# Turned input, normalization behind the products, and a first block with k outermost

## The reference

```python
h = x
proj = rmsnorm(h, norm_mix_g) @ w_in          # 512 x 1024 @ 1024 x 4624
y_a = gmlp_chunk_mixer(proj[:, :2048], ...)   # gelu, per-head rmsnorm of v, 128x128 causal mixing, rmsnorm
y_b = ssd_mixer(proj[:, 2048:], ...)          # z | x,B,C -> causal conv (4 taps) -> silu | dt -> softplus; scan
h = h + concat([y_a, y_b]) @ w_out
h = h + square(relu(rmsnorm(h, norm_mlp_g) @ w_ff1)) @ w_ff2
h = h + sigmoid(rmsnorm(h, ple_norm_g) @ w_gate) * (p @ w_ple)
out = rmsnorm(h, final_norm_g)

rmsnorm(x, g) = x * rsqrt(mean(x * x) + eps) * g
```

## Time and profile before

| | us |
|---|---|
| median of 3 runs (733.01 to 733.64) | 733.08 |
| span of the profiled execution, first to last instruction | 731.3 |
| median less span (what lies around the span) | 1.8 |
| PE busy | 721.8 |
| DVE busy | 528.3 |
| ACT busy | 410.3 |
| POOL busy | 134.1 |
| start of the first matmul of block 0 | 10.99 |
| granted TensorE clock, mean | 0.997 |

### The profile page before, as it was taken

How to read it: one execution, slowest core, us unless ns; L and a number is a source line. 1 busy time by engine, 2 the same in 40 slices (tenths; PEclk the granted TensorE clock), 3 DMA queues, 4 the chain that set the end, 5 groups by cost and what they waited for, 6 DMA issues and landing times.

```text
span 731.3 us, 9961 instructions
## 1 busy us (share of the span) xinstructions
PE 721.8 (99%) x3962; PEld 622.3 (85%) x3962; DVE 528.3 (72%) x552; ACT 410.3 (56%) x521; POOL 134.1 (18%) x112
## 2 busy tenths in 40 slices
PE   8999999999999999999999999999999999999996
PEld 7888887778887888888899889988999889988884
DVE  5556795477658555555889985899579967898874
ACT  6534456653576762413767742774447625673875
POOL 1021000756645000001110211212111121020000
PEclk9999999999999999999999999999999999999998
DMA  8632222343233153219667898889978997887311
GB/s 330 205 105 86 87 87 89 115 151 109 86 111 120 60 201 116 73 43 285 151 170 211 178 296 159 218 192 295 206 180 222 221 250 156 235 177 260 115 58 58
DMA packets 52229, 118.24 MB, mean 162 GB/s; under 512 B 5052, under 2 KB 5208, under 8 KB 52184
## 3 DMA queue, kind: packets, MB, share of 16 engines
q1 hardware_dynamic: 39816, 84.03, 34.4%
q0 software_dynamic: 11136, 29.36, 22.1%
q10 hardware_dynamic: 1232, 4.23, 1.8%
HBM read 96.60 MB, written 4.23 MB: 138 GB/s over the span
## 4 chain that ended last, share of the span: by engine, by line
PE 97%; DMA 1%; DVE 1%; ACT 1%; issue 0%; SPq 0%
PE acc L1651 28%; PE acc L1653 28%; PE acc L1652 28%; PE side L1716 3%; PE side L1651 2%; PE side L1652 2%; PE side L1653 2%; PE side L1809 2%; PE side L1776 1%; DMA w_raw<-in_w_in 1%; PE side L1816 1%; PE side L1804 1%; DVE w_lo L1108 0%; PE side L1756 0%; PE side L1757 0%; PE side L1796 0%
## 5 line engine op out<-in xcount | busy, mean ns | idle before, releaser
L767 ACT ACTIVATE ring_hi<-quarter 128x1024 fp32r<-128x1024 f32 x112 | 113.6, 1051 | 101.9 <-PE acc L1653 46.5
L1409 DVE TENSOR_TENSOR ring_lo<-quarter,ring_hi 128x1024 fp32r<-128x1024 f32 x112 | 132.8, 1219 | 38.0 <-ACT ring_hi L767 37.7
L1651 PE MATMUL acc<-w_hi,a_hi 128*128 128x512 f32 x256 | 104.4, 408 | 0.1
L1653 PE MATMUL acc<-w_hi,a_lo 128*128 128x512 f32 x256 | 100.1, 391 | 0.0
L1652 PE MATMUL acc<-w_lo,a_hi 128*128 128x512 f32 x256 | 99.8, 390 | 0.0
L648 POOL DMA_DIRECT2D quarter<-in_w_ff x24 | 29.2, 1236 | 240.4 <-DMA quarter<-in_w_ff 240.2
L1652 PE MATMUL acc<-xS_lo,ring_hi 128*128 128x256 f32 x256 | 72.4, 283 | 0.0
L1108 DVE TENSOR_TENSOR w_lo<-w_raw,w_hi 128x1024 fp32r<-128x1024 f32 x36 | 48.0, 1336 | 27.1 <-ACT w_hi L669 26.7
L1651 PEld LDWEIGHTS acc<-w_hi,a_hi 128*128 128x128 f32 x256 | 48.1, 188 | 11.5 <-issue 1.4
L1652 PEld LDWEIGHTS acc<-w_lo,a_hi 128*128 128x128 f32 x256 | 48.2, 188 | 10.7 <-issue 1.4
L1653 PEld LDWEIGHTS acc<-w_hi,a_lo 128*128 128x128 f32 x256 | 48.0, 188 | 10.4
(11 more groups left out here) (290 smaller groups left out, 1817.7 us busy)
## 6 DMA issues: line engine op xcount, KB each, us to landing
quarter<-in_w_ff SPq DMA_DIRECT2D x72, 512.0 KB, 5.8
w_raw<-in_w_in SPq DMA_DIRECT2D x36, 512.0 KB, 3.7
quarter<-quarter POOLq DMA_DIRECT2D x32, 512.0 KB, 8.0
quarter<-in_w_ff POOLq DMA_DIRECT2D x24, 512.0 KB, 7.4
w_raw<-in_w_out SPq DMA_DIRECT2D x16, 512.0 KB, 3.5
h<-in_x SPq DMA_DIRECT2D x8, 512.0 KB, 4.7
seg<-cs_dram ACTq DMA_DIRECT2D x8, 512.0 KB, 3.8
w_raw<-in_w_ple_gate SPq DMA_DIRECT2D x8, 512.0 KB, 5.7
```

Of the source, the lines that this page charges most:

```text
L767: act.activation(ring[n % 3][0][at], quarter[i][at], ACT.Copy).then_inc(form_hi, 1)
L1409: dve.tensor_tensor(lo[at], src, hi[at].bitcast(F32), ALU.subtract).then_inc(form_lo, 1)
L1651: pe.matmul(dst, st[0], mv[0], start=start, stop=False)
L1653: return pe.matmul(dst, st[1], mv[0], start=False, stop=stop)
```

## The change

x comes a second time from DRAM, turned (channels on partitions), into the space of `y`, eight pieces of 128 channels by 512 tokens, and `norm_mix_g` as a small tile with one gain for each channel (`g_col`). a_hi and a_lo are made from these two with no turning on PE and no token factor. The token factors come from x as before, into `rstd`, and are applied behind the products: as the scale of gelu and silu in blocks V, U and Z, and in blocks 2 to 4 by a DVE multiplication with a tile `rstd_row` that holds them along the free dimension on every partition. That tile is made by one matmul of ones by four diagonal matrices behind group 4, and copied out by ACT at t = 6. Block 0 runs with k as the outer loop over its four banks. ACT issues the first three weight pieces of block 0, SP the other five and the eight of x turned. WARM is 11, REWARM is gone; `ones` is set by DVE.

```diff
+            for k in range(KT):                                    # SP
+                sp.dma_start(xt_raw[:, k, :], xt_dram[:, k, :]).then_inc(xt_landed[k], 16)
+                if k == 0:
+                    sp.dma_start(g_col[:], a["norm_mix_g"]).then_inc(g_col_landed, 16)
+                if k >= ACT_FIRST:
+                    sp.dma_start(w_raw[:, k // 2, k % 2, :], w_in[:, k, W:W + 512]).then_inc(first_landed[k], 16)
+            for s in range(NS):
+                load_x(s)
...
+            for k in range(ACT_FIRST):                             # ACT
+                act.dma_start(w_raw[:, k // 2, k % 2, :], w_in[:, k, W:W + 512]).then_inc(first_landed[k], 16)
             act.wait_ge(eps_ready, 1)
             act.activation(early_rms[:], eps[:], ACT.Sqrt).then_inc(sqrt_loaded, 1)
+            act.wait_ge(g_col_landed, 16)
+            for k in range(KT):
+                split_xt(k)      # a_hi[:, k, :] = xt_raw[:, k, :] * g_col[:, k]
+                split_first(k)   # w_hi[:, 0, k, :] = w_raw
+            for s in range(NS):
+                sums(0, s)
+            for p in range(4):
+                split_hi(1, p)
...
+                if t == 6:
+                    freed(act.activation(rstd_row, wait_full(act, "rstd_row"), ACT.Copy), "rstd_row")
...
-                    act.activation(conv[:, i % 2, :], acc[:, s, :], ACT.Copy, scale=cols[:, 36 + i:37 + i]
+                    act.wait_ge(*emptied(b, s))
+                    act.activation(conv[:, i % 2, :], tmp[:, i % 2, :], ACT.Copy, scale=cols[:, 36 + i:37 + i]
                                    ).then_inc(conv_begun, 1)
-                    act.wait_ge(*emptied(b, s))
+                    act.wait_ge(conv_step, 3 * i + 3)
...
+            for k in range(KT):                                    # DVE
+                split_xt(k)      # a_lo
+                split_first(k)   # w_lo
+            dve.wait_ge(consts_ready, 2)
+            for s in range(NS):
+                dve.wait_ge(rms_ready, s + 1)
+                dve.reciprocal(rstd[:, s:s + 1], rms[:, s:s + 1]).then_inc(rstd_ready, 1)
+                dve.wait_ge(rstd_ready, s + 1)
+                dve.tensor_scalar(rstd_diag[:, s, :], ident[:], rstd[:, s:s + 1], None, ALU.mult
+                                  ).then_inc(diag_ready, 1)
+            for p in range(4):
+                split_lo(1, p)
...
             for t in range(4 * OUT):                               # DVE
                 b, s = divmod(t, 4)
-                if 1 <= t < 3:
-                    xt_evac(0, t + 1)
+                if 5 <= t < 9:
...                      # the v_ssq reduction, moved to the head of the iteration
+                if t == 11:
+                    bank = wait_full(dve, "dt")
+                    freed(dve.tensor_tensor(dtT[:], bank[0:2 * R, :], rstd_row[0:2 * R, :], ALU.mult), "dt")
+                if X <= b < U:
+                    i = t - 4 * X
+                    dve.wait_ge(acc_full, t + 1)
...
+                    dve.tensor_tensor(tmp[:, i % 2, :], acc[:, s, :], rstd_row, ALU.mult).then_inc(dve_evac, 1)
                 if t == 16:
                     bank = wait_full(dve, "decay")
                     dve.tensor_copy(cs[:], bank[:, 0:NS * R]).then_inc(cs_ready, 1)
...
                     freed(dve.tensor_copy(csT[:], bank[0:NS * R, 0:P]), "csT")
...
-                split_lo(b + 1, s)
+                if b:
+                    split_lo(b + 1, s)
...
-                        ins = dve.scalar_tensor_tensor(dst, acc[:, s, 0:SEQ - k], w, dst, ALU.mult, ALU.add)
+                        dve.scalar_tensor_tensor(dst, tmp[:, i % 2, 0:SEQ - k], w, dst, ALU.mult, ALU.add
+                                                 ).then_inc(conv_step, 1)
...
+            def first_block():                                     # PE
+                for k in range(KT):
+                    pe.wait_ge(xa_lo, k + 1)
...                      # and w_lo of slice k
+                    for s in range(NS):
+                        at = (slice(None), k, slice(s * P, s * P + P))
+                        ins = product(acc[:, s, :], [t[at] for t in (a_hi, a_lo)],
+                                      [t[:, 0, k, :] for t in (w_hi, w_lo)], k == 0, k == KT - 1)
+                        if k == KT - 1:
+                            ins.then_inc(acc_full, 1)
...
+                if t == 4:
+                    bank = open_bank("rstd_row")
+                    pe.wait_ge(diag_ready, NS)
+                    filled(pe.matmul(bank, ones[:], rstd_diag.rearrange("p s n -> p (s n)"), start=True, stop=True),
+                           "rstd_row")
...
                 if t == 11:
                     bank = open_bank("dt_nat")
-                    wait_free(pe, "dt")
+                    pe.wait_ge(dt_biased, 1)
```

## The result

The changed kernel takes **744.5 us** (four runs, 743.0 to 744.7) against 733.05 us before: a ratio of 1.0151, interval [1.0136, 1.0165]. The forecast was 733.2 with a range to 735.6, so the time lies 11.3 us above the one and 8.9 above the other. The profiled execution took 744.46 us, with a span of 742.7. The difference to explain is 742.7 - 731.3 = 11.4 us of span.

What follows compares the result with a forecast made beforehand. PE was taken to bound the kernel (97% of the 731.3 us span). Terms -8.0 + 0.9 + 1.0 + 0.5 + 0.4 + 1.4 + 3.9 = +0.1 gave span 731.4, with 1.8 to the median 733.2 us; range 730.8 to 735.6.

Steps and rivals of the forecast that it cites:

- Start and end of block 0: Block 0: first product at 6.4 (range 6.0 to 7.2), 4.6 us earlier; its end 8.0 us earlier.
- rival 1: Block 0's start: the array still or again at the lower clock level, at most 2.25 us more, 735.5; chance 0.18.
- rstd_row: One fp32 matmul of 128x512 on PE to make the tile of token factors: 0.9 us more.
- Waits behind 13, 14 and 15: PE waits for silu before the turnings behind these groups, DVE being later: 1.0, 0.5 and 0.4 us.
- Behind group 16: PE's last turning waits for the bank behind DVE's multiplication, cs copy and ACT's exp: 1.4 us.
- The sum it led to, 1.9: The wait at t = 16 if a drain of 1.38 us follows each table load: 1.9 us, left out of the forecast.
- Behind group 17: Mix products wait for ACT's copy, behind DVE's multiplication and late csT copy: 3.9 us, the largest wait.
- From t = 18 on ACT is level again: Iterations from t = 18: ACT has caught up, split and two mix copies done before group 18 ends; no wait added.
- Rival 4: DVE lags further at t >= 19 beside POOL, or g_col is late: 1.5 to 2.5 us more, 735.2; chance 0.10.
- The price of a wait: Waits of PE behind groups 13 to 17: each added at its own length only, S = 7.2 us in all.

Runs made afterwards that it cites:

- Experiment 4: The changed kernel with ACT's two waits ahead of the exp of decay (t = 16) in the other order, cs_ready first: 741.6 us.
- Experiment 3: The kernel before the change, with one wait added: at t = 17 DVE waits for acc_full ahead of the csT copy: 738.12 us.
- experiment 2: The changed kernel with only the csT copy (t = 17) put back ahead of the wait for acc_full and the multiplication: 740.5 us.
- Experiment 1: The changed kernel with DVE's cs (t = 16) and csT (t = 17) copies put back ahead of the acc_full wait and multiplication: 737.2 us.
- experiment 6: The changed kernel with the multiplication in place in PSUM: 740.6 us; with the cs and csT copies also ahead of the acc_full wait: 731.1 us.
- experiment 9: The changed kernel with cs, csT and dts work ahead, multiplication in PSUM, and GpSimd's first seg subtraction behind VectorE's split (t = 18): 728.59 us.
- experiment 8: The changed kernel with cs, csT and dts work ahead and multiplication in PSUM, with 16 or 6 warming pairs instead of 11: 730.2 and 731.2 us.

## Why the prediction was wrong, step by step

**Start and end of block 0: right in kind, 2.6 us too good.** The first product was forecast at 6.4 (range to 7.2) and came at 7.01. `g_col` was taken to land at 4.3; a_hi began at 4.68, 3.4 us behind the issue at 1.25, near the upper bound of 3.8. Then came the half pace of rival 1: the array idled 0.82 us before the first product, and eight intervals of 0.43 instead of 0.23 cost 1.7 us, inside the 2.25 given as its most. That isn't regular: seven further kernels with the same 11 pairs began block 0 at the full level in their profiled execution, though idle for 0.85 to 1.79 us ahead of it. The rest is the turning of `cols`, which in the kernel before stood inside block 0 (30.69) and now stands behind it (30.51, 0.35 us until the products are level again): 8.0 - 0.6 - 1.7 - 0.35 = 5.35, for 5.4 measured.

**rstd_row: right.** Lag -5.4 to -4.5 us, 0.9 as forecast.

**Waits behind 13, 14 and 15: right.** 1.1, 0.4 and 0.4, for 1.0, 0.5 and 0.4.

**Behind group 16: the first failed step, 1.4 forecast, 2.9 measured.** The term added the multiplication, the copy and the exp. It put the table load ahead of the wait because that is where the row of the kernel before had it; there ACT came to it with nothing left to wait for. Experiment 4 shows the missing 1.3 us. The rule weighed at this place, a drain of 1.38 us with each load ("ScalarE: Activation LUTs", section "What ACT_TABLE_LOAD costs", in the Trainium skill), was rightly set aside: the exp starts 0.02 us behind the end of the load (115.57 + 1.28, then 116.87). The sum it led to, 1.9, was nearer than 1.4, for another reason.

**Behind group 17: right, 3.9 forecast and measured.** Experiment 3 confirms the mechanism with that one instruction alone, and experiment 2 removes it.

**"From t = 18 on ACT is level again": the second failed step, 3.7 us.** It counted ACT's own work and took DVE's taps at 2.31 us although the change moves their operand from PSUM to SBUF. Beside GpSimd they took 4.42 us and the split ahead of them 2.68, so silu, split, mix copies and b_nat came late. Rival 4 had named the place ("t >= 19 ... beside POOL") but not the mechanism, and gave it 1.5 to 2.5 us and a chance of 0.10. Experiment 1 shows that it doesn't hang on the earlier waits, experiment 6 that the operand's place decides what the taps cost: 2.31 us from PSUM beside the same GpSimd work. That is 2.0 of the 3.5 us of wait in the changed kernel, and with the copies ahead all 4.3. The rest fits the split, which stands in both kernels with two inputs in SBUF; it is argued from its 2.75 us against 1.22, and experiment 9, where GpSimd is put behind it, has no such wait. A page that I had not weighed states this: the Trainium skill, "SBUF — State Buffer", section "SBUF: two separate sides", has it that a VectorE instruction with two SBUF inputs and a GpSimd one that reads SBUF hold a shared port pair for the whole instruction, and that the loser blocks. The traces agree, to within 0.15 us in the two sums of experiment 8.

**The price of a wait: the third failed step, 3.4 us.** The sum gave each wait its own length. The array's level was thought of as a matter of the start alone. Behind the waits of 3.7 and 3.5 us the granted clock was 0.66 over 5 us, 1.7 us each; experiment 3 shows it with one wait of 3.1 us (5.0 us in the median, 1.75 of it behind the wait).

Together: 2.6 at the start (8.0 less 5.4), 1.5 behind group 16, 3.7 behind 19 and 3.4 of clock are 11.2 of the 11.3 us by which the median missed the forecast. Two of these causes had stood among the rivals, each with a chance for itself; that both could come on top of the forecast, with a further cost in clock for each long wait, was not in the range.

## What to carry to other kernels

Multiplying behind a product instead of ahead of it moves work behind the group's end: whatever else stands behind that wait on the same engine should be moved ahead of it first (here 744.5 to 737.2 us). Look at where each operand lies when an instruction of VectorE runs beside one of GpSimd, and keep one tensor operand in PSUM where it was made (to 731.1 us); where both must be in SBUF, give them an order (728.6 us, four of five executions within 0.4 us). A wait of TensorE of 3 to 4 us in a busy stretch, as here, should be priced at its length and 1.4 to 1.8 us more.

## What the runs showed of the hardware that was not expected

- Two engines at SBUF: VectorE's 128x1024 split of two SBUF tensors takes 1.22 us alone and 2.67 when GpSimd's instruction of 1.90 was first; GpSimd's takes 2.61 when VectorE was first. Three taps took 2.31 us alone, 4.42 and 6.64 beside GpSimd, and 2.31 beside GpSimd with one operand in PSUM. Where a load's landing decided the order, profiled executions differed by 1.5 to 1.7 us in it.
- A table load stands behind the wait that was written last of two: 2.71 or 1.37 us of wait for PE, by the order of two lines.
- Each of the ten profiled waits of TensorE of 3.1 to 4.3 us between groups was followed by a stretch of 5 us with a granted clock of 0.66 to 0.81, and by the starts on PE each cost 1.4 to 1.8 us on top of its length. Behind a wait of 2.7 us that was so in one of four profiled executions.
- At the start of the kernel the granted clock of the profile reads 1.00 while matmuls start 0.43 us apart, the pace of the lower level.
